# A sparse layer's scores on the full array, two small linears in one, an index linear by rows, and a new order of all work

## The reference, cut to what matters

```python
# even layer: which keys a query may see
rel = jax.nn.relu(jnp.einsum('bqhd,bsd->bqhs', qib, k_idx))      # 4 index heads of 64
score = jnp.einsum('bqh,bqhs->bqs', wb, rel)
_, sel = lax.top_k(score, topk)                                  # 64 of 256

# sparse layer: one key head of 64 for 12 query heads, three branches with a gate each
q, kc, vc, ks, vs, kw, vw, g, qm = split_cols(x @ a_w_in[i], A_IN_SIZES)
lg = jnp.einsum('bqgjd,bgqkd->bqgjk', qc, ks) * scale + bias_s   # selected blocks
p_s = masked_softmax(lg, dist_s >= 0)
lg = jnp.einsum('bqgjd,bkgd->bqgjk', qc, kw) * scale + bias_w    # window
p_w = masked_softmax(lg, mask_w)
o = gc[..., 0:1] * o_c + gc[..., 1:2] * o_s + gc[..., 2:3] * o_w # o_c: compressed keys
```

## Time and profile before

| | us |
|---|---|
| median of 3 runs | 866.23 (866.14 to 866.57) |
| span of the profiled execution | 864.6 |
| TensorE busy in it | 855.4 (99%) |
| VectorE busy | 671.9 (78%) |
| ScalarE busy | 489.5 (57%) |
| GpSimd busy | 40.3 (5%) |
| DMA engines, mean share | tenths 1 to 9, 179 GB/s |

### The profile page before, as it was taken

How to read it: one execution, slowest core, us unless ns; L and a number is a source line. 1 busy time by engine, 2 the same in 40 slices (tenths; PEclk the granted TensorE clock), 3 DMA queues, 4 the chain that set the end, 5 groups by cost and what they waited for, 6 DMA issues and landing times.

```text
span 864.6 us, 13438 instructions
## 1 busy us (share of the span) xinstructions
PE 855.4 (99%) x5062; PEld 725.5 (84%) x5062; DVE 671.9 (78%) x1238; ACT 489.5 (57%) x905; POOL 40.3 (5%) x72
## 2 busy tenths in 40 slices
PE   9999999999999999999999999999999999999997
PEld 7888888888888878788888888888888888888885
DVE  4889887868886788988776867887768787677876
ACT  5584375668775776655555445545664565544541
POOL 0105000110001100000000000000000000000000
PEclk9999999999999999999999999999999999999999
DMA  9775526467436861235566556537344456566641
GB/s 328 287 240 150 167 80 194 137 221 222 167 99 228 268 219 49 77 111 179 172 202 212 174 193 228 188 131 251 115 159 146 146 195 221 169 220 213 216 155 49
DMA packets 46748, 155.12 MB, mean 179 GB/s; under 512 B 5500, under 2 KB 8668, under 8 KB 46684
## 3 DMA queue, kind: packets, MB, share of 16 engines
q1 hardware_dynamic: 41408, 141.39, 48.9%
q10 hardware_dynamic: 5276, 12.88, 4.9%
HBM read 152.38 MB, written 1.34 MB: 178 GB/s over the span
## 4 chain that ended last, share of the span: by engine, by line
PE 97%; DVE 1%; ACT 1%; DMA 0%; issue 0%; SPq 0%; POOL 0%; DVEq 0%
PE ps L2161 17%; PE ps L2189 14%; PE ps L797 12%; PE ps L973 10%; PE ps L2169 9%; PE ps L809 6%; PE ps L861 5%; PE ps L872 4%; PE ps L864 4%; PE ps L1062 4%; PE ps L1119 3%; PE ps L1071 3%; PE ps L905 1%; PE ps L800 1%; PE ps L801 1%; DMA raw<-in_ws 0%
## 5 line engine op out<-in xcount | busy, mean ns | idle before, releaser
L769 DVE TENSOR_TENSOR wlo<-raw,whi 128x1024 fp32r<-128x1024 f32 (+1 forms) x262 | 311.1, 1216 | 56.6 <-ACT whi L762 55.3
L762 ACT ACTIVATE whi<-raw 128x1024 fp32r<-128x1024 f32 x261 | 266.6, 1049 | 115.9 <-DMA raw<-in_ws 37.1
L2161 PE MATMUL ps<-t,whi 128*128 128x512 f32 x640 | 156.1, 391 | 0.0
L2161 PEld LDWEIGHTS ps<-t,whi 128*128 128x128 f32 x640 | 117.7, 188 | 22.8
L797 PE MATMUL ps<-t,whi 128*128 128x512 f32 x432 | 109.3, 397 | 0.0
L2189 PE MATMUL ps<-whi,r 128*128 128x512 f32 x352 | 95.4, 391 | 0.0
L797 PEld LDWEIGHTS ps<-t,whi 128*128 128x128 f32 x432 | 78.2, 188 | 17.3 <-issue 1.8
L2169 PEld LDWEIGHTS ps<-t,wlo 128*128 128x128 f32 x640 | 84.7, 191 | 4.7
L2169 PE MATMUL ps<-t,wlo 128*128 128x256 f32 x640 | 86.4, 283 | 0.0
L2189 PEld LDWEIGHTS ps<-whi,r 128*128 128x128 f32 x352 | 64.6, 188 | 12.2
L809 PEld LDWEIGHTS ps<-t,wlo 128*128 128x128 f32 (+1 forms) x472 | 62.5, 189 | 4.2 <-issue 0.3
(11 more groups left out here) (277 smaller groups left out, 1149.4 us busy)
## 6 DMA issues: line engine op xcount, KB each, us to landing
raw<-in_ws SPq DMA_DIRECT2D x251, 512.0 KB, 4.5
vecs<-in_vecs ACTq DMA_DIRECT2D x12, 512.0 KB, 4.6
arena<-in_ws ACTq DMA_DIRECT2D x5, 512.0 KB, 7.5
raw<-in_ws SPq DMA_DIRECT2D x8, 256.0 KB, 5.6
raw<-in_ws SPq DMA_DIRECT2D x4, 416.0 KB, 4.3
tb<-brow ACTq DMA_DIRECT2D x8, 192.0 KB, 4.3
rows<-in_mem SPq DMA_DIRECT2D x4, 256.0 KB, 5.2
x<-in_x SPq DMA_DIRECT2D x1, 1024.0 KB, 7.6
```

Source lines behind the costliest of these rows:

```text
L762: a.i.activation(whi[:, j % NSPLIT, 0:n], raw[:, j % NRAW, 0:n], ACT.Copy).then_inc(*a.sig("hi", u))
L769: d.i.tensor_tensor(wlo[:, j % NSPLIT, 0:n], raw[:, j % NRAW, 0:n], whi[:, j % NSPLIT, 0:n].bitcast(F), ALU.subtract).then_inc(*d.sig("lo" ...
L2161: p.i.matmul(ps[:, b, :], wh[:, k, :], t2[:, k, :], start=k == 0, stop=False)
```

## The change

1. `e_idx` becomes a chunk of 324 columns (three units of 972, 972 and 648 elements a partition). ScalarE writes its rows to `irows`, with the key columns twice, and the weights to `iw` at once. A step `index` makes six transposes of 128x128, in two banks `e_ix`, and ScalarE copies them to `iqT` and `ikT`. `iw` on TensorE and VectorE goes.
2. `a_c` goes as a linear: its 256 columns are appended to `a_v`, now 420 columns in four units of two blocks each. ScalarE copies the 256 columns of each half to `crows`; a step `crows` makes four transposes into one bank; the steps `tile a_c` evict from there, as before with four copies each.
3. The sparse layer's scores are in fp32r. For each pair of heads ScalarE writes the high half of the queries to one half of the partitions of a stack and VectorE the rest to the other half, for both heads (`stack 0` to `stack 5`). `kk_hi` and `kk_lo` hold the keys' halves, each twice. Two matmuls, stack times `kk_hi` and stack times `kk_lo`, over all 128 partitions, make both sets of scores of one head. The stacks lie in memory that `small`, `kc2` and `vc2`, and `rows` have at other times, and `kk_lo` in that of `bc`.
4. `cen a`, the first part of the layer norm, waits for the last scores, as `rows` holds stacks.
5. All lists of `ORDER` are new, of every stage. The steps in them are the same but for those named above.

```diff
-    tiles("e_idx", e, span(2048, 256) + span(2304, 64) + span(2368, 4))
+    chunk("e_idx", e, span(2048, 256) + span(2304, 64) + span(2368, 4))
...
-    chunk("a_v", a, span(960, 64) + span(1088, 64) + span(1152, 36))
-    tiles("a_c", a, span(768, 128) + span(896, 64) + span(1024, 64))
+    chunk("a_v", a, span(960, 64) + span(1088, 64) + span(1152, 36) + span(768, 128) + span(896, 64) + span(1024, 64))
...
-    in_turn(*both("a_v"), *each("a_c"), *each("a_qm"), *each("a_q"), n=2)
+    in_turn(*both("a_v"), "a_c", *each("a_qm"), *each("a_q"), n=2)
...
+    def pe_log_stacked(p, g):
+        p.wait_ge("key_lo", 0)
+        for t in range(g.h0 // 2, (g.h0 + g.n) // 2):
+            p.wait_ge("stack_lo", t)
+        for i in range(g.n // 2):
+            for s in range(2):
+                q_ = stacks[g.h0 // 2 + i][:, s, g.q * P:g.q * P + P]
+                o = ps[:, g.banks[s], 2 * g.W * i:2 * g.W * (i + 1)].rearrange("p (z w) -> p z w", z=2)
+                p.i.matmul(o, q_, kk_hi[:, :, 0:g.W], start=True, stop=False)
+                mm = p.i.matmul(o, q_, kk_lo[:, :, 0:g.W], start=False, stop=True)
+    def act_stack(a, t):
+        a.wait_ge(*ready("a_q", t))
+        if t == 1:
+            a.wait_ge("blk", 1, 1)
+        elif t >= 2:
+            a.wait_ge("w1", w1_units[4 + (t - 2) // 2])
+        for s in range(2):
+            o = slice(64 * s, 64 * s + 64)
+            last = a.i.activation(stacks[t][o, s, :], N["qT"][o, t, :], ACT.Copy)
+    def dve_stack(d, t):
+        d.wait_ge("stack_hi", t)
+        for s in range(2):
+            o, other = slice(64 * s, 64 * s + 64), slice(64 - 64 * s, 128 - 64 * s)
+            last = d.i.tensor_tensor(stacks[t][other, s, :], N["qT"][o, t, :], stacks[t][o, s, :].bitcast(F), ALU.subtract)
+    def dve_key_rest(d):
+        d.wait_ge("ev", "a_c", 1)
+        pv = ps[:, BANK["a_c"], T:2 * T]
+        for z in range(2):
+            k = slice(64 * z, 64 * z + 64)
+            for s in range(2):
+                last = d.i.tensor_tensor(kk_lo[64 * s:64 * s + 64, z, :], pv[k, :], kk_hi[k, z, :].bitcast(F), ALU.subtract)
...
+            elif what == "crows":
+                b = BANK["a_c"]
+                p.fill(b, ("ev", "a_c", 0), ("key_lo", 0))
+                for q in range(2):
+                    p.wait_ge("crows", q)
+                    for t in range(2):
+                        mm = p.i.transpose(ps[:, b, t * T + q * P:t * T + q * P + P], N["crows"][:, q, t * P:t * P + P], ident[:, :])
```

More of the change, by code:

```diff
@@ L290 @@
+        lo 2, gated d2, mix e 2, lo 1, mix e 3, outlo d2, lo 3, gain post0 0 0, gain post0 0 1, xw e 0 0, xw e 0 1, lo 1,
+        row pre1 0 0, row pre1 0 1, lo 2, T 3 0 0, gain post0 1 0, gain post0 1 1, xw e 1 0, xw e 1 1, T 3 0 1, lo 1,
+        row pre1 1 0, row pre1 1 1"""),
         pool=listed("""
@@ L328 @@
         pe=listed("""
-        chunk a_v 0 0, clow a_v 0 0, chunk a_v 1 0, clow a_v 1 0, T 5 1 0, T 5 1 1, chunk a_v 0 1, chunk a_v 1 1, clow a_v 0 1,
-        clow a_v 1 1, tile a_c 0, tlow a_c 0, tile a_c 1, tlow a_c 1, tile a_qm 0, tlow a_qm 0, tile a_qm 1, tlow a_qm 1, w1 k 0, w1 k 1,
-        w1 k 2, log m0, tile a_q 0, tile a_q 1, log m1, tlow a_q 0, tlow a_q 1, turn m0 0, turn m0 1, w1 k 3, w1 v 0, w1 v 1, w1 v 2,
-        w1 v 3, log n0, tile a_q 2, tlow a_q 2, log n1, comp1, tile a_q 3, tlow a_q 3, turn m1 0, turn m1 1, log n2, val m0, comp3,
@@ new lines @@
+        proj a 5 1, turn n8 0, plow a 5 1, plow a 4 1, proj a 6 1, val n8, T 7 0 0, plow a 6 1, proj a 7 1, T 7 0 1"""),
+        act=listed("""
+        hi 1, T 5 1 0, w1load 4, hi 1, T 5 1 1, w1load 5, gte 0, crows 0, hi 1, crows 1, gte 1, tile a_c 0, tile a_c 1, hi 1,
+        half a_qm 0, hi 2, w1load 6, w1load 7, hi 1, half a_qm 1, hi 1, half a_q 0, hi 1, exp m0 0, exp m0 1, stack 0,
+        half a_q 1, hi 1, stack 1, comp0, exp m1 0, exp m1 1, half a_q 2, hi 1, exp n0 0, exp n0 1, hi 1, stack 2, exp n1 0,
@@ new lines @@
+        T 7 0 1"""),
+        dve=listed("""
+        T 5 1 0, lo 2, T 5 1 1, vsw 0, lo 1, vsw 1, lo 1, blocks, key, lo 2, sum a_qm 0, gate0 0, lo 1, sum a_qm 1, lo 2,
+        mask m0 0, mask m0 1, lo 1, sum a_q 0, mul m0, mask m1 0, sum a_q 1, stack 0, lo 1, stack 1, mask m1 1, mul m1,
+        mask n0 0, mask n0 1, lo 1, sum a_q 2, gate0 1, pt m0, mask n1 0, mask n1 1, mul n0, mask n2 0, sum a_q 3, stack 2,
+        mul n1, mask n2 1, sum a_q 4, stack 3, outlo m0, pt m1, pt n0, comp2, mul n2, comp3, mask n3 0, sum a_q 5, mask n3 1,
@@ L486, in sb, with beside @@
         return ctx.enter_context(nc.sbuf_tensor(name, shape, dt))
+    def beside(name, shape):
+        with nc.sbuf_tensor(name, shape, R) as v:
+            return v
     raw = sb("raw", [P, NRAW, UNIT])
@@ L580, in _build @@
     N["hrow"] = N["pcT"].rearrange("p q n -> p (q n)")[:, 0:512]
+    N["crows"] = N["hrow"].rearrange("p (q n) -> p q n", q=2)
+    stack1, kk_hi = (arena_r[:, at:at + 2 * T].rearrange("p (s n) -> p s n", s=2) for at in (8 * T, 10 * T))
+    stacks = [stack0[:, :, :], stack1] + [in_rows[:, t, :, :] for t in range(4)]
     A = Area()
@@ L853, in pe_chunk @@
                 p.fill(b, ("lora", q), ("krows", q))
+            elif name == "a_v":
+                p.fill(b, ("ev", "a_v", q), ("crows", q))
             else:
@@ L2028, in act_nsa @@
                 a.i.activation(N["gte"][:, q, :], ps[:, BANK["a_v", q], 128:164], ACT.Exp, scale=-1.0).then_inc(*a.sig("ev", "a_v", q))
+            elif what == "crows":
+                q = k[0]
+                a.wait_ge("evd", "a_v", q)
+                a.i.activation(N["crows"][:, q, :], ps[:, BANK["a_v", q], 164:420], ACT.Copy).then_inc(*a.sig("crows", q))
             elif what == "comp0":
@@ L2050, in act_nsa @@
                 act_out(a, "a", *k)
+            elif what == "stack":
+                act_stack(a, *k)
             else:
@@ L2126, in dve_nsa @@
                 dve_out(d, "a", *k)
+            elif what == "stack":
+                dve_stack(d, *k)
+            elif what == "key":
+                dve_key_rest(d)
             else:
```

423 lines of the change are left out of this document (222 added, 201 removed).

## The result

The changed kernel takes 876.72 us (876.28 to 877.73, 4 runs) against 866.19 us (866.14 to 866.57, 4 runs): ratio 1.0119, interval 1.0105 to 1.0134. It is 10.5 us slower; 863.0 was predicted, with 860.3 to 866.6 as the range.

A forecast was written before the change was run, and what follows sets the result against it. TensorE, busy 99% of the span, was taken as the bound. Its work was to shrink 5.4 us; waits of +0.9, +0.3, +1.0, -0.5 and +0.5 left -3.2, from 866.23 to 863.0 us, range 860.3 to 866.6.

The forecast's parts named there:

- Index linears: Even layer: 48 matmuls of 324 columns at 0.148 and six transposes replace three tiles, -1.05 us, bounds -1.9 and 0.
- Sparse layer: Small linears -1.6 us; stacked scores add 0.6, fewer array-shape borders save 2.35; waits at new-row transposes removed, -0.5.
- Rivals D and E: Stacked scores at the plain fp32 price, 870.1 (0.03); 420 columns priced as 512 and 324 at 0.17, 865.9 (0.03).
- The added waits named in advance: Sparse layer, TensorE waits before three steps: `crows` +0.9 us, `w1 k 0` +0.3, `tile a_qm 1` +1.0.
- rival A: The added waits, 2.2 us, and VectorE's share of 0.5 are covered by other work: 860.3 us, chance 0.22.
- VectorE near 95% and no TensorE wait for it: Expected sign late in the sparse layer: VectorE's 16 added subtractions, 5.6 us, fit into its 8.0 us free.
- The +0.5 charged: Sparse layer: the part of VectorE's added 5.6 us of subtractions expected to show, bounds 0 to +5.6.
- rival C: VectorE becomes the bound of the sparse stage and all 5.6 us of added subtractions show: 868.1 us, chance 0.07.
- The new order elsewhere: outside the start hardly a wait is left to remove: Reordered steps in the other stages: with TensorE 99% busy, effect taken as 0, bounds -2 to +3 us.
- so I charge no wait: Even layer, between `index` and the score step: 3.7 us of TensorE work covers ScalarE's 2.5; at most 1.
- Rival B: All stages: the new order loses the gain, 30 steps each 0.1 us late, 866.0 us, no difference; chance 0.15.
- So no clock enters the sum: Whole kernel: the granted clock is full in every slice of the profile before, so no clock cost was counted.

The follow-up runs named there:

- `index_only`: The kernel before with only the index columns computed by rows and turned, its own order otherwise: 868.59 us, ratio 1.0023.
- `sparse_only`: The kernel before with only the changed sparse layer, its linears, stacked scores and order: 868.13 us, ratio 1.0018.
- `filled19`: The changed kernel with 19 throwaway matmuls in the wait ahead of the first retention score step: 874.66 us, ratio 1.0094.
- `rot_dve`: The changed kernel with VectorE's sum of the last rotated tile moved ahead of the second score: 871.31 us, ratio 1.0052.
- `sparse_light`: The kernel before with the changed sparse layer, its value, memory query and query weight loads cut to an eighth: 866.33 us, ratio 0.9994.
- `order_only`: The kernel before with only the new order of the odd layer, last attention layer and both feed-forward parts: 868.66 us, ratio 1.0032.
- `rot_early`: The changed kernel with the last rotated tile's low pass, half and sum moved earlier on TensorE, ScalarE and VectorE: 871.12 us, ratio 1.0049.
- `both_fix`: The kernel before with the changed even layer, three places mended, and the changed sparse layer, one ScalarE weight split earlier: 872.67 us, ratio 1.0072.

## Why the prediction was wrong

The sum had two halves. The half on TensorE's own work was right:

- Index linears: -1.05 predicted, -0.85 measured (`index_only`). The 324 columns cost 0.148, as taken.
- Sparse layer: linears -1.6 and its share of the scores and borders, 2.35 - 0.6, -3.35 together, and -0.5 for transposes, -3.85; between -3.6 and -4.2 measured (`sparse_only`). Stacked scores cost 0.12 and 0.23, 420 columns 0.19. Rivals D and E fall.
- The added waits named in advance: `crows` +0.9 (0.69 over its floor), `w1 k 0` +0.3 (0.36), `tile a_qm 1` +1.0 (0.97). 2.0 for 2.2. They are not covered, so rival A falls too.
- VectorE near 95% and no TensorE wait for it: it is busy 93%, but TensorE waits 0.96 us for it late in the layer, 0.61 of it at the compressed scores. The +0.5 charged was half of that; rival C, with all 5.6 us, falls.

The half that failed is the step "The new order elsewhere: outside the start hardly a wait is left to remove", taken as 0, and with it "so I charge no wait" in the even layer. It asked what an order can remove where TensorE never waits, and not what it can add, and it weighed ScalarE and VectorE and never named GpSimd, busy 5%. Its bounds of -2 to +3 were too narrow as well. Rival B had the direction, that the new order loses what the shorter work gains, but put it at 30 steps of 0.1 us, spread out. The runs showed something else: one producer off the chain with 5.8 us of slack, made 8.3 us late by its release and its length and wanted 2.0 earlier. In the even layer the changed kernel pays 4.6 for it (4.47 of idle and the hand-over), about 4.1 for the clock that falls behind it (`filled19`), and 1.4 for VectorE's rows behind a split: 10.1, less 0.85, is the +9.3 of the table. `rot_dve` shows that one step's place in VectorE's list carries more than half of the +9.3.

"So no clock enters the sum" rested on a page where the clock was full; that was no ground for the kernel after, since the clock followed the wait.

In the sparse layer the unnamed waits were larger than the named: 1.64 at the second memory score step, 0.48 at the first stacked scores, 0.34 and 0.41 later, 2.9 in all, and the 0.61 at the compressed scores. ScalarE stood 3.08 us for a load and the chain went on through it (ScalarE's rows, then VectorE's):

```profile
315.01 1.06 ACT L795 ACTIVATE whi<-raw 128x1024 fp32r<-128x1024 f32 x1 [3.08 <-DMA raw<-in_ws]
...
317.96 0.47 ACT L1266 ACTIVATE sm<-ps,stat 128x256 f32<-128x256 f32 x1 [0.64 <-DVE stat L1250]
...
316.10 1.23 DVE L802 TENSOR_TENSOR wlo<-raw,whi 128x1024 fp32r<-128x1024 f32 x1 [1.85 <-ACT whi L795]
317.24 1.28 DVE L1250 TENSOR_REDUCE stat<-ps 128x2 f32<-128x512 f32 x2
```

ScalarE's split comes first, VectorE's split behind it, and only then the maxima (line 1250) and exponentials (line 1266) on which the score step waits. The prediction checked ScalarE's and VectorE's free time, and not that the layer's weights, with less TensorE work to cover them, come later than they are wanted (`sparse_light`, 1.0 us).

Sizes against the kernel before: even layer +9.3 (in the changed kernel), sparse +1.3 (`sparse_only`), order elsewhere +2.1 when alone (`order_only`). They sum to 12.7, against 10.2 behind the start in the table. Of `order_only`'s 2.1 nearly all are three waits in the sparse layer's old order, 0.42, 0.31 and 1.11 of idle time, and the changed kernel has none of them. What remains open: why waits of 0.94 (`rot_dve`) and 1.86 (`rot_early`) lowered the clock and waits of 0.93 (`rot_early`) and 3.22 (`both_fix`) did not; and whether an order exists in which both shorter parts show, since none of the mended orders did it.

## What to carry to other kernels

Where the bound engine never waits, look at the engines off the chain for how late each may come: list every producer's end beside the time at which it is wanted, before a written order is changed, since a slack of 5.8 us is invisible in the chain and in the busy shares. Work taken off the bound engine makes everything else due earlier, loads too, and a step placed behind a waiting split in an in-order queue inherits that wait. Price a long wait of TensorE as the gap, and count with as much again for the clock behind it: behind 4.47 us that was 4.05, behind 3.22 in `both_fix` nothing, so this second price is a range and not a sum. Where a GpSimd step stands beside a run of VectorE's splits, reckon that it may end only with that run.
